# Two tiles of the input projection cut into three pieces each instead of four, in a decoder layer on one core

## The reference: what is computed

```python
x = x + 0.5 * swiglu_ffn(x, ...)
h = rms_norm(x, mix_norm)
gq, gk, gv, gz, ga, gb, mq, mk, mv, cq = split(h @ w_in)
y_gdn  = gated_deltanet(gq, gk, gv, gz, ga, gb, ...)   # 4 heads x 128, delta rule in chunks
y_moba = moba_attention(mq, mk, mv, ...)               # 4 heads x 64, block-sparse, causal
y_mem  = memory_attention(cq, rms_norm(mem), ...)      # 4 heads x 64, 256 memory tokens
x = x + concat(y_gdn, y_moba, y_mem) @ w_out
x = x + 0.5 * swiglu_ffn(x, ...)
```

## Time and profile before

| | us |
|---|---|
| median of 3 runs | 995.43 (995.32 to 995.48) |
| the profiled execution | 995.95 |
| its span, first to last instruction | 993.9 |
| TensorE busy in it | 988.6 (99%) |
| VectorE, GpSimd, ScalarE busy | 687.1, 503.7, 441.4 |

### The profile page before, as it was taken

How to read it: one execution, slowest core, us unless ns; L and a number is a source line. 1 busy time by engine, 2 the same in 40 slices (tenths; PEclk the granted TensorE clock), 3 DMA queues, 4 the chain that set the end, 5 groups by cost and what they waited for, 6 DMA issues and landing times.

```text
span 993.9 us, 16353 instructions
## 1 busy us (share of the span) xinstructions
PE 988.6 (99%) x6761; PEld 870.7 (88%) x6761; DVE 687.1 (69%) x1093; ACT 441.4 (44%) x647; POOL 503.7 (51%) x289
## 2 busy tenths in 40 slices
PE   9999999999999999999999999999999999999998
PEld 7888999999999988788877888888899999999997
DVE  6894976676666487853647874788598776667746
ACT  7642444344443462534456764533254334443341
POOL 0355865676656433543152301646476675756741
PEclk9999999999999999999999999999999999999999
DMA  8432322332223312321221001322312333123312
GB/s 311 155 128 80 127 86 86 128 128 95 76 85 128 127 43 85 127 85 48 80 87 44 3 2 44 126 86 85 128 44 86 127 128 114 57 86 128 128 42 86
DMA packets 15913, 95.31 MB, mean 96 GB/s; under 512 B 2016, under 2 KB 2400, under 8 KB 5600
## 3 DMA queue, kind: packets, MB, share of 16 engines
q1 hardware_dynamic: 15696, 94.23, 26.5%
q10 hardware_dynamic: 144, 0.05, 0.0%
HBM read 92.17 MB, written 2.10 MB: 95 GB/s over the span
## 4 chain that ended last, share of the span: by engine, by line
PE 98%; DVE 1%; issue 0%; ACT 0%; POOL 0%; DVEq 0%; POOLq 0%
PE bank L1996 56%; PE bank L2122 32%; PE bank L2174 1%; PE bank L2435 1%; PE bank L2439 1%; PE bank L2549 1%; PE bank L2483 1%; PE bank L2521 0%; PE bank L2538 0%; PE bank L2461 0%; PE bank L2495 0%; PE bank L2385 0%; PE bank L2601 0%; PE bank L2505 0%; PE bank L2392 0%; PE bank L2579 0%
## 5 line engine op out<-in xcount | busy, mean ns | idle before, releaser
L2122 PE MATMUL bank<-t_ffn_hi,wlo 128*128 128x256 f32 x896 | 253.6, 283 | 0.0
L2122 PE MATMUL bank<-t_ffn_lo,whi 128*128 128x256 f32 x896 | 253.6, 283 | 0.0
L2122 PE MATMUL bank<-t_ffn_hi,whi 128*128 128x256 f32 x896 | 253.5, 283 | 0.0
L511 POOL TENSOR_TENSOR wlo<-raw,whi 128x1024 fp32r<-128x1024 f32 (+1 forms) x42 | 142.1, 3400 | 180.9 <-ACT whi L608 164.3
L528 POOL TENSOR_TENSOR wlo<-sums,whi 128x512 fp32r<-128x512 f32 x128 | 170.5, 1353 | 120.8 <-ACT whi L733 120.6
L528 POOL TENSOR_TENSOR wlo<-raw,whi 128x512 fp32r<-128x512 f32 x96 | 158.6, 1666 | 37.8 <-ACT whi L733 37.7
L2122 PEld LDWEIGHTS bank<-t_ffn_hi,whi 128*128 128x128 f32 x896 | 172.0, 192 | 0.6
L2122 PEld LDWEIGHTS bank<-t_ffn_lo,whi 128*128 128x128 f32 x896 | 172.0, 192 | 0.6
L2122 PEld LDWEIGHTS bank<-t_ffn_hi,wlo 128*128 128x128 f32 x896 | 172.0, 192 | 0.0
L1996 PE MATMUL bank<-ahi,whi 128*128 128x512 f32 x428 | 169.2, 395 | 0.0
L1996 PE MATMUL bank<-ahi,wlo 128*128 128x512 f32 x428 | 166.9, 390 | 0.0
(11 more groups left out here) (339 smaller groups left out, 1408.9 us busy)
## 6 DMA issues: line engine op xcount, KB each, us to landing
raw<-fast_in SPq DMA_DIRECT2D x32, 1024.0 KB, 4.9
raw<-stream SPq DMA_DIRECT2D x29, 1024.0 KB, 4.9
raw_down<-fast_in SPq DMA_DIRECT2D x18, 1024.0 KB, 7.0
raw<-stream SPq DMA_DIRECT2D x7, 512.0 KB, 8.0
out<-x SPq DMA_DIRECT2D x7, 256.0 KB, 2.0
x<-x_in SPq DMA_DIRECT2D x3, 512.0 KB, 9.0
memx<-mem_in SPq DMA_DIRECT2D x2, 512.0 KB, 11.3
raw_gate<-stream SPq DMA_DIRECT2D x1, 1024.0 KB, 4.9
```

Of the source, the lines that this page charges most:

```text
L511: ins = nc.gpsimd.tensor_tensor(wlo[:, u % RING, c0:c1], raw_unit(u)[:, c0:c1], whi[:, u % RING, c0:c1].bitcast(F32), ALU.subtract)
L2122: ins = E.matmul(psum[bank][:, HALF * h:HALF * (h + 1)], a, b[:, k, :], start=start and k == 0 and m == 0, stop=k == K2 - 1 and m == 2, sk ...
```

## The change

TensorE's order alone is edited. Tile 24's last two pieces (blocks 4 to 6 and 6 to 8) become one piece ahead of level_second(0, 3). Tile 25's last two become one piece ahead of mk_spread(1); the second of them stood between level_first(0, 5) and mem_turn(4). The matmuls, their operands and all waits stay as they were.

```diff
             mem_scores(4)
             level_first(0, 3)
-            in_part(24, 11, 0, 4, 6)
+            in_part(24, 11, 0, 4, 8)
             level_second(0, 3)
-            in_part(24, 11, 0, 6, 8)
             mem_turn(2)
             level_first(0, 4)
             mk_turn()
...
             mem_turn(3)
-            in_part(25, 11, 1, 4, 6)
+            in_part(25, 11, 1, 4, 8)
             mk_spread(1)
             level_second(0, 4)
             mem_out(3)
             mem_scores(5)
             level_first(0, 5)
-            in_part(25, 11, 1, 6, 8)
             mem_turn(4)
```

## The result

| | before | changed kernel |
|---|---|---|
| median of 6 runs, us | 995.49 (995.32 to 996.12) | 1000.09 (999.32 to 1002.15) |
| ratio, 95% interval | | 1.0047 (1.0037 to 1.0057) |
| profiled execution: time, span | 995.95, 993.9 | 999.32, 997.5 |

What follows compares the result with a forecast made beforehand. TensorE's own work plus its waits was taken as the bound. +1.37 + 1.37 = +2.74 us moves the profiled execution from 995.95 to 998.69; the median lies 0.52 lower, forecast 998.1, range 996.8 to 999.0.

Steps and rivals of the forecast that it cites:

- The pieces in themselves: Six matmuls added to a TensorE piece cost 1.37 us; the passages saved are some 0.2 us for both places.
- First place, level_first(0, 4)'s wait: After level_second(0, 3), TensorE waits some 0.4 us for level_update; some 0.35 us to show as idle.
- First place, mk_turn: VectorE's chain from level_second(0, 3) keeps its 3.78 us, so mk_turn starts at 522.68, +1.37 us.
- Second place: Six more matmuls ahead of mk_spread(1) make level_second(0, 4) and mem_turn(4) another 1.37 us later, +2.74 us in all.
- What comes behind: After mem_turn(4) all engines are equally late; TensorE's waits of 0.81 and 0.4 us absorb none of the delay.
- The clock: TensorE's granted clock stays at 1.00, 2.4 GHz, as at its existing 0.81 us idle; no clock cost counted.
- rival 3: TensorE's clock falls after a new idle; one such stretch costs 2.7 us more, 1000.9. Chance 0.03.
- Rival 1: Only one of the two places' chains decides: +1.4 us, 996.8. Chance 0.10.
- rival 2: At mk_turn and mem_turn(4) the moved matmuls were no cover; only saved passages remain, -0.2 us, 995.2. Chance 0.06.

Runs made afterwards that it cites:

- mask_late: The changed kernel with GpSimd's mask for level_first(0, 5) held back until VectorE has scaled the norms; 998.77 us, ratio 1.0030.
- second_only: The kernel before with only tile 25's pieces merged; 997.01 us against 995.77, ratio 1.0014.
- first_only: The kernel before with only tile 24's pieces merged; 1001.17 us, ratio 1.0046.
- idle_alone: idle_without_port with GpSimd's following weight split held back until mk_scale(0) is done; 1000.99 us, ratio 1.0050.
- first_mask_late: first_only with GpSimd's mask for level_first(0, 5) held back; 997.03 us, ratio 1.0014.
- idle_without_port: mask_late with two more memsets of 64x512 on VectorE ahead of the norms; 1002.50 us, ratio 1.0071.

## Why the prediction was right or wrong

- **The pieces in themselves** (1.37 us more ahead of each level_second): right. 518.90 in before's time, as forecast.
- **First place, level_first(0, 4)'s wait**: right, 0.29 us shown where I had 0.35.
- **First place, mk_turn: the step that failed.** "+1.37 us" came from VectorE's chain keeping its 3.78 us. It took 4.79, since the chain had moved under GpSimd's mask. The term should have been 1.37 + 1.02 = 2.4. I had dealt with GpSimd in one sentence, about the mask that level_first(0, 4) waits for, and not asked what the next mask would stand beside once VectorE is late. mask_late put a number on it: without the overlap the chain and the sum are as recorded. The range failed with the term: no bound of it let a chain grow, and its upper end was 1.49 + 1.53 with the wait of 0.40 at level_first(0, 4) added once more, which is already part of the 1.49. Even the four executions whose clock held lie above 999.0.
- **Second place** (+1.37): right, 1.40 in the changed kernel, 1.2 alone in second_only. GpSimd took nothing from its chain in either kernel. In the changed kernel the weight split was over (525.49 + 4.75 = 530.24) when level_second(0, 4) started at 530.98. In the kernel before it ran from 525.76 for 4.57 us, beside the first 2.2 us of VectorE's work from level_update(0, 4) on (528.16). There VectorE had only operations with a PSUM bank as an input (L1725, L1668, L1735, L1770) and one of a single element (L1736), and each took what it takes in the changed kernel (L1725 0.75, L1668 0.74). My working did not look at this either: here it was luck.
- **What comes behind**: right. The waits of 0.8 and 0.4 us stayed and took up nothing.
- **The clock: the choice that failed.** I gave rival 3 a chance of 0.03 and a price of 2.7 us. The price was of the right size (2.9 in first_only's trace, 1.6 in idle_alone's). The chance was not: 5 of the changed kernel's 11 executions. I had argued from one idle of 0.81 us without a fall, to idles for which I myself forecast 0.9 and 1.4. At these lengths it did hold (0 of 28 executions of mask_late, first_mask_late and second_only), so with the chain at 3.78 us the forecast would have stood. The blocked operation made the idle 1.9 us, and in the kernels with one idle of 1.9 or 2.2 it fell in 13 of 21. One missed term brought in the other.
- **The two together**: +3.6 us in span in the profiled execution, and 1.6 and 2.8 more in the two whose clock fell. These two lie above the rest and so lift the median of six from 999.54 to 1000.09; what is left of the way from 3.6 to 4.6 is of the size by which the time outside the span varies (2.1 and 2.8 us in the two middle executions, 1.8 in the profiled one).
- **Rival 1** (one place only) and **rival 2** (the matmuls were no cover): both wrong. The two waits were there and added up.

What stays open: why the clock falls in some executions and not in others of the same kernel, and why the low stretch is longer in one than in another. No run here separates them.

## What to carry to other kernels

When an edit makes one engine late, list what every other engine does in the stretch that it moves into; for VectorE, that is each GpSimd operation that could now start first, and the price, where VectorE's operation reads two tiles of SBUF or is of the kind that was blocked here, was the rest of that GpSimd operation, whatever the VectorE operation's size. A line whose longest time is many times its median (here 4.51 us against 0.18 for L1151) is the sign to look for ahead of the edit. Work placed between a producer and its consumer is cover: moving it costs its full length where the chain beside it has no slack, and a matmul engine idle for two us may cost 1.6 to 2.9 more by its clock, as in the two traces here.

## What the runs showed of the hardware that I had not expected

- A VectorE operation of 0.19 us on two SBUF operands took 1.21 us beside a GpSimd operation of 1.26, and one of 0.35 us with a single tile in SBUF as input took 4.50 beside one of 4.55. Each ended within 0.2 us of the GpSimd operation's end, which had begun first by 0.10 and 0.20 us.
- Kernels with one idle of TensorE of 1.9 or 2.2 us had a mean clock under 1.000 in some executions and not in others: 13 of 21 (with idle_without_port, which has a second one of 2.6 us, 17 of 26). Both traces of such executions show a stretch at the 1.2 GHz level behind the idle. Kernels whose longest new idle is 0.9 or 1.4 us had none, in 28.
- The low stretch began at the end of the idle in one trace (clock 0.80 from 523 to 524, with mk_turn at 523.87, first_only) and 1.5 us after it in the other, when TensorE worked again (matmuls 0.42 to 0.43 us apart from 524.93 on, mk_turn at 523.46, idle_alone).
- Thirteen matmuls with no use went with a clock of 1.000 in all five executions (999.33 us in the median, where the changed kernel had 1000.09 and 1000.71); how much time this gives back is not shown beyond the noise.
